# Output projection of a differential-attention layer as seven block products over token pairs, column halves and the two k-tiles of a head

## The reference

```python
mod = silu(c) @ ada_w + ada_b; shift, scale, gate = split(mod, 3)
h = rms_norm(x, norm_pre) * (1 + scale) + shift
q, k, v, z = h @ w_in                    # 8 heads, v 256 wide, q and k 2 x 128 wide
p = softmax(where(mask, q k^T / sqrt(128), -1e30))      # for each of two maps
o = (p[0] - lam * p[1]) @ v              # mask: key chunk <= query chunk (64)
o = rms_norm(o, subln) * 0.8 * silu(z)   # per head
y = o @ w_out                            # 1024 x 2048 times 2048 x 2048
out = x + gate * rms_norm(y, norm_post)
```

## Time and profile before

| | |
|---|---|
| three executions | 1976.6, 1975.08, 1976.04 us; median 1976.04 |
| the profiled execution, its own time | 1976.31 us |
| its span, first to last instruction | 1974.5 us |
| mean granted TensorE clock | 0.994 |
| TensorE busy | 98% of the span |
| HBM read / written | 295.75 / 128.98 MB |

### The profile page before, as it was taken

One profiled execution on the slowest core, in us unless ns is written; L12 is line 12 of the kernel. 1 busy time (PEld: TensorE's weight loads), 2 busy tenths in 40 slices (PEclk: granted clock), 3 DMA queues, 4 the chain that ended last, 5 costly groups with the idle time before them and its releaser, 6 DMA issues.

```text
span 1974.5 us, 26574 instructions
## 1 busy us (share of the span) xinstructions
PE 1927.3 (98%) x9222; PEld 1579.9 (80%) x9222; DVE 1294.4 (66%) x2118; ACT 787.2 (40%) x1567; POOL 567.1 (29%) x624
## 2 busy tenths in 40 slices
PE   4999999999999999999999999999999999999998
PEld 1378888888888888888888888888888878888886
DVE  2776766666556446788788888888788745434352
ACT  4533333333444333444444444444444434322240
POOL 2033333423456324232332434332332310000000
PEclk8999999999999999999999999999999999999999
DMA  9777666563556777776768687777768675377453
GB/s 327 249 242 238 211 195 214 189 215 103 183 177 216 273 275 257 234 251 208 242 195 261 203 241 229 233 238 217 238 200 257 234 256 171 112 256 210 153 154 85
DMA packets 398353, 426.51 MB, mean 216 GB/s; under 512 B 21158, under 2 KB 295692, under 8 KB 396044
## 3 DMA queue, kind: packets, MB, share of 16 engines
q1 hardware_dynamic: 397936, 424.77, 67.8%
q10 hardware_dynamic: 284, 0.05, 0.0%
HBM read 295.75 MB, written 128.98 MB: 215 GB/s over the span
## 4 chain that ended last, share of the span: by engine, by line
PE 89%; SPq 3%; DMA 2%; DVE 2%; POOL 2%; issue 1%; ACT 1%; DVEq 0%; POOLq 0%; ACTq 0%
PE ps L1620 28%; PE ps L1622 28%; PE ps L1621 28%; PE ps L1752 2%; PE ps L1603 1%; POOL stg L766 1%; PE ps L1726 1%; POOL sums L745 1%; SPq L507 1%; PE ps L1771 1%; DMA h_dr<-stg 1%; PE ps L1588 1%; SPq L393 1%; DMA q_sb<-q_dr 0%; DMA x2s<-in_x_dram 0%
## 5 line engine op out<-in xcount | busy, mean ns | idle before, releaser
L1620 PE MATMUL ps<-blk,ring 128*128 128x512 f32 x1524 | 602.8, 396 | 5.8 <-issue 2.3
L1622 PE MATMUL ps<-blk,ring 128*128 128x512 f32 x1524 | 594.1, 390 | 0.0
L1621 PE MATMUL ps<-blk,ring 128*128 128x512 f32 x1524 | 593.7, 390 | 0.0
L1620 PEld LDWEIGHTS ps<-blk,ring 128*128 128x128 f32 x1524 | 286.3, 188 | 64.6 <-issue 6.8
L1622 PEld LDWEIGHTS ps<-blk,ring 128*128 128x128 f32 x1524 | 286.0, 188 | 60.8
L1621 PEld LDWEIGHTS ps<-blk,ring 128*128 128x128 f32 x1524 | 286.5, 188 | 55.8
L1149 DVE TENSOR_TENSOR ring<-sums,ring 128x512 fp32r<-128x512 f32 x256 | 225.8, 882 | 127.7 <-ACT ring L849 125.4
L745 POOL TENSOR_TENSOR sums<-raw 128x512 f32<-128x512 f32 x128 | 192.8, 1506 | 346.7 <-DVE ring L1149 262.8
L849 ACT ACTIVATE ring<-sums 128x512 fp32r<-128x512 f32 x256 | 160.0, 626 | 173.5 <-PE ps L1622 171.3
L1149 DVE TENSOR_TENSOR ring<-raw,ring 128x512 fp32r<-128x512 f32 x192 | 163.6, 853 | 80.9 <-ACT ring L849 79.8
L745 POOL TENSOR_TENSOR sums<-sums,raw 128x512 f32<-128x512 f32 x128 | 190.5, 1488 | 24.8 <-DVE ring L1149 17.7
(11 more groups left out here) (161 smaller groups left out, 3039.4 us busy)
## 6 DMA issues: line engine op xcount, KB each, us to landing
raw<-in_diff_w_in_dram SPq DMA_DIRECT2D x64, 1024.0 KB, 7.2
w_raw<-in_diff_w_out_dram SPq DMA_DIRECT2D x128, 256.0 KB, 3.9
d_dr<-cc SPq DMA_DIRECT2D x124, 256.0 KB, 2.7
cc<-d_dr SPq DMA_DIRECT2D x124, 256.0 KB, 3.9
ada<-in_ada_w_dram SPq DMA_DIRECT2D x92, 256.0 KB, 7.1
ada<-in_ada_w_dram SPq DMA_DIRECT2D x32, 512.0 KB
q_sb<-q_dr SPq DMA_DIRECT2D x64, 256.0 KB, 3.2
k_sb<-k_dr SPq DMA_DIRECT2D x64, 256.0 KB, 3.9
```

Of the source, the lines that this page charges most:

```text
L1620: MM(dst, a_hi, b_hi, start=start, stop=False, skip_group_check=True)
L1621: MM(dst, a_hi, b_lo, start=False, stop=False, skip_group_check=True)
L1622: return MM(dst, a_lo, b_hi, start=False, stop=stop, skip_group_check=True)
```

## The change

The output projection is written as block products over pairs of token tiles (2p and 2p+1), halves of 512 columns inside each column half c of 1024, and the two k-tiles of a head. With A the gated output of a head in blocks (token tile, k-tile) and B a head's rows of `w_out` in blocks (k-tile, 512 columns), each head needs seven products:

- P1 = A11 B11, P2 = A12 B21, P3 = (A12 - S2) B22, P4 = A22 T4, P5 = S1 T1, P6 = S2 T2, P7 = S3 T3
- S1 = A21 + A22, S2 = S1 - A11, S3 = A11 - A21
- T1 = B12 - B11, T3 = B22 - B12, T2 = B22 - T1, T4 = B21 - T2
- Y11 = P1 + P2, Y12 = P1 + P6 + P5 + P3, Y22 = P1 + P6 + P7 + P5, Y21 = P1 + P6 + P7 + P4

A unit is one product of one head for all four token pairs, again 12 matmuls of 128x512. The table `OUT` gives the order: per column half P1, P6, P7, P4, P5, P3, P2, each over the heads. P6, P7, P4 and P3 go on in the bank of the product before (`GOES_ON`); after P1, P6, P7 and P4 the bank is copied to `y` by ScalarE (p even) and VectorE (p odd), after the others VectorE adds the bank to `y`. In the first column half the last head is left out of the seven and done as eight plain products (K11, K12, K21, K22, two units each). So there are 7 x 7 + 8 + 7 x 8 = 113 units.

The sums S are made by POOL (`o_sums`, four 128x128 operations per pair, in all heads) and stored unsplit with A in `s_dr` (`store_pair`); the splits and stores of `oz` are gone. The sums T are made by POOL in place (`t_sum`, four 128x512 operations per head and column half) and stored in `t_dr`: for c = 0 in the first half of the input products, one head per 14 products, for c = 1 in the last head's attention (`T_AT`) and after it. The load of x's second half comes after the first of these passes, from product 116 on. A unit's two operands, weights and A, 128x512 each, are loaded together into one of `UR` = 10 buffers and split together, 128x1024 (`unit_high`, L1114; `unit_low`, L1526), `made_by(u) - u` units ahead: 2 until unit 38, rising to 8 from unit 59 on. The squares are taken from `y`, and POOL multiplies `y` by `gpb` (`L927`). In the last product (P2 of c = 1) TensorE goes pair by pair, 24 matmuls each.

```diff
-    OUTS = 2 * GROUPS * KT
...
+    PAIRS = TT // 2
+    K12, K11, K21, K22 = range(NP, NP + 4)
+    OUT = [(0, (P1,), 0), (0, (P6,), 0), (0, (P7,), 0), (0, (P4,), 0), (0, (P5,), 0), (0, (P3, K12), 0),
+           (0, (P2, K11), 1), (0, (K21,), 0), (0, (K22,), 1),
+           (1, (P1,), 0), (1, (P6,), 0), (1, (P7,), 0), (1, (P4,), 0), (1, (P5,), 1), (1, (P3,), 1), (1, (P2,), 0)]
+    GOES_ON = (P6, P7, P4, P3)
+    COPIED = (P1, P6, P7, P4)
+    TO = {P1: (0, 0), P2: (0, 0), P6: (0, 1), P3: (0, 1), P7: (1, 1), P5: (1, 1), P4: (1, 0), K21: (1, 0), K22: (1, 1)}
+    UNIT = [(q, c, op, u) for q, (c, ops, _) in enumerate(OUT) for op in ops
+            for u in range(2 if op >= NP else HEADS - (c == 0))]
+    OUTS = len(UNIT)
+    BEGIN = [min(n for n in range(OUTS) if UNIT[n][0] == q) for q in range(len(OUT))]
+    END = [max(n for n in range(OUTS) if UNIT[n][0] == q) for q in range(len(OUT))]
+    LAST = len(OUT) - 1
...
+    UR = 10
+    LEAD = 2
...
+    T_AT = {0: 0, 2: 1, 3: 2, 4: 3, 5: 4, 6: 5, 7: 6}
...
+        def made_by(n):
+            return min(OUTS - 1, n + LEAD + min(6, max(0, (n - BEGIN[5]) // 4))) if n >= 0 else n + LEAD
...
+            def store_pair(h, p):
+                sp.wait_ge(ozf_ok, h * NB + 2 * p + 2)
+                sp.dma_start(s_dr[0:4, h, :, p].rearrange("o p n -> p o n"),
+                             ozf.rearrange("p i m n -> p (i m) n")).then_inc(s_st, 16)
+                sp.wait_ge(osum_ok, 4 * (h * PAIRS + p + 1))
+                sp.dma_start(s_dr[4:8, h, :, p].rearrange("o p n -> p o n"), osum[:, :, :]).then_inc(s_st, 16)
...
+            def load_unit(n):
...
+                    sp.wait_ge(unit_used, n - UR + 1)
+                if op in (P5, P7, P4, P6):
+                    t = (P5, P7, P4, P6).index(op)
+                    sp.wait_ge(t_st[u % 2], 32 * ((c * HEADS + u) // 2 + 1))
+                    src = t_dr[c, u, t]
...
+                sp.dma_start(ubf[k][:, 1, 0], src).then_inc(unit_in[k], 16)
+                if op >= NP:
+                    s, h = 2 * (op in (K21, K22)) + u, LH
+                else:
+                    s, h = {P1: 0, P2: 1, P4: 3, P5: 4, P6: 5, P7: 6, P3: 7}[op], u
+                sp.wait_ge(s_st, 32 * PAIRS * (h + 1))
+                sp.dma_start(ubf[k][:, 1, 1], s_dr[s, h].rearrange("p t n -> p (t n)")).then_inc(unit_in[k], 16)
...
+            while n < BEGIN[5] + HEADS - 1:
+                load_unit(n)
+                n += 1
+            store_t(1, HEADS - 2)
+            load_t(1, HEADS - 1)
+            store_pair(LH, PAIRS - 1)
+            while n < OUTS:
+                load_unit(n)
+                n += 1
+                if n == BEGIN[6]:
+                    store_t(1, HEADS - 1)
+                t, r = divmod(n - BEGIN[9] - UR, 4)
+                if r == 0 and 0 <= t < TT:
+                    if t == 0:
+                        for e in range(2):
+                            sp.wait_ge(t_st[e], 32 * HEADS)
+                    load_x(XT[t])
...
+            def o_sums(a):
+                n = 4 * (a // 2)
+                a11, a12, a21, a22 = ozf[:, 0, 0], ozf[:, 0, 1], ozf[:, 1, 0], ozf[:, 1, 1]
+                pool.wait_ge(ozf_ok, a + 1)
+                TTP(osum[:, 0], a21, a22, ALU.add).then_inc(osum_ok, 1)
+                TTP(osum[:, 2], a11, a21, ALU.subtract).then_inc(osum_ok, 1)
+                pool.wait_ge(osum_ok, n + 1)
+                TTP(osum[:, 1], osum[:, 0], a11, ALU.subtract).then_inc(osum_ok, 1)
+                pool.wait_ge(osum_ok, n + 3)
+                TTP(osum[:, 3], a12, osum[:, 1], ALU.subtract).then_inc(osum_ok, 1)
...
+                if qb == NB - 1:
+                    o_sums(HEADS * NB - 1)
+                if qb in T_AT:
+                    for step in range(4):
+                        t_sum(1, T_AT[qb], step)
...
+            def unit_high(n):
+                act.wait_ge(unit_in[n % UR], 32 * (n // UR + 1))
+                A(ub[n % UR][:, 0], ubf[n % UR][:, 1], ACT.Copy).then_inc(unit_hi, 1)
+            def make(u):
+                for n in range(made_by(u - 1) + 1, made_by(u) + 1):
+                    unit_high(n)
...
+            def read_out(q, p):
+                to, bank = y_block(q, p), ps[:, out_bank(q, p)]
+                dve.wait_ge(*made(q, p))
+                if OUT[q][1][0] in COPIED:
+                    i = V.tensor_copy(to, bank)
...
-            def tiles_done(u):
+                    c, ops, _ = OUT[q]
+                    old = max(r for r in range(q) if OUT[r][0] == c and TO[OUT[r][1][0]] == TO[ops[0]])
+                    dve.wait_ge(*read[old, p])
+                    i = TTV(to, bank, to, ALU.add)
+                i.then_inc(y_d, 1)
...
+            def unit(n, p):
+                q, c, op, u = UNIT[n]
+                new = n == BEGIN[q] and OUT[q][1][0] not in GOES_ON
+                s = slice(p * P, (p + 1) * P)
+                return three(ps[:, out_bank(q, p)], ub[n % UR][:, 0, 1, s], ub[n % UR][:, 1, 1, s],
+                             ub[n % UR][:, 0, 0], ub[n % UR][:, 1, 0], new, n == END[q])
+            def bank_waits(q, p):
+                if on_bank[q] is not None:
+                    pe.wait_ge(*read[on_bank[q], p])
+                elif p == 0 and q:
+                    pe.wait_ge(ozf_ok, HEADS * NB)
+                elif p == 0:
+                    pe.wait_ge(ev_d, 3 * GP + NP * GP)
...
+            def tick(n):
+                q = UNIT[n][0]
+                pe.wait_ge(unit_ok, n + 1)
+                for p in range(PAIRS):
+                    if n == BEGIN[q]:
+                        bank_waits(q, p)
+                    last = unit(n, p)
+                    if n == END[q] and p < PAIRS - 1:
+                        last.then_inc(op_done, 1)
+                last.then_inc(unit_used, 1)
...
+            for p in range(PAIRS):
+                read_out(LAST, p)
+                col = (2 + TO[P2][1]) * HALF
+                dve.wait_ge(*read[LAST, p])
+                TTV(y_end[:, p], y_block(LAST, p), gpb[:, col:col + HALF], ALU.mult).then_inc(y_end_ok, 1)
+                if p == 0:
+                    finish(1, PAIRS - 1)
+                y_sum(0, slice(p, p + 1), SQ[LAST, p] + 1)
+                finish(0, p)
```

More of the change, by code:

```diff
@@ L86, in build @@
     ADA_BUF = list(range(14)) + [0, 1, 2, 3, 4, 5, 6, 7, 8, 9, 0, 1, 2, 3, 4, 5, 0, 1]
-    assert GC == UK * P
-    assert END[EARLY] >= sum(map(sum, SLOTS)) > END[EARLY - 1]
+    T_PASS = 14
+    assert BEGIN[6] > sum(map(sum, SLOTS)) + 8 and OUT[6][2] == 1
     ctx = ExitStack()
@@ L220, in build @@
+        y_end = at("y_end", [P, PAIRS, HALF], F32, [e_at + BLK // 2 * 3])
+        assert (OUTS - HEADS - 1) % UR == 4 and max(x_places) + BLK // 2 <= nc.sbuf_usable_end
+        for used in (base, a_at, b_at, z_at):
             assert used[0] <= nc.sbuf_usable_end, (used[0], nc.sbuf_usable_end)
@@ new lines, in _ @@
+            while n < OUTS:
[4 more added lines that the diff above has]
+                t, r = divmod(n - BEGIN[9] - UR, 4)
+                if r == 0 and 0 <= t < TT:
+                    if t == 0:
+                        for e in range(2):
+                            sp.wait_ge(t_st[e], 32 * HEADS)
+                    load_x(XT[t])
+            for p in range(PAIRS):
+                t = 2 * p + 1
+                sp.wait_ge(fin, 2 * p + 2 if p < PAIRS - 1 else 2 * PAIRS)
+                sp.dma_start(out[0, t * P:(t + 1) * P, :], xt[t][:, :]).then_inc(out_st, 16)
@@ L719, in _ @@
+            for p in range(PAIRS):
+                t = 2 * p
+                for k, (b, e) in enumerate(((0, 1024), (1536, 2048), (1024, 1536))):
+                    sp.wait_ge(fin, 2 * PAIRS + 3 * p + k + 1)
+                    sp.dma_start(out[0, t * P:(t + 1) * P, b:e], xt[t][:, b:e]).then_inc(out_st, 16)
+            sp.wait_ge(out_st, 4 * PAIRS * 16)
         @block.gpsimd
@@ new lines, in tick, with y_sum, finish @@
+            def tick(u):
+                if u in END:
+                    q = END.index(u)
+                    for p in range(PAIRS):
+                        if read[q, p][0] is y_d:
+                            read_out(q, p)
+            def y_sum(i, pairs, done):
+                dve.wait_ge(yss_ok, done)
+                V.tensor_reduce(out=yms[:, i, pairs], in_=yss[:, i, pairs], axis=AX.X, op=ALU.add).then_inc(yms_ok, 1)
+            def finish(i, p):
+                t = 2 * p + i
+                if i == 1 and p == 0:
+                    dve.wait_ge(xh_in, 16 * TT)
+                dve.wait_ge(yrs_ok, 1 if i else p + 2)
+                dve.wait_ge(yg_ok, SQ[LAST - 2 if i else LAST - 1, p] + 1)
+                r = yrs[:, i, p:p + 1]
+                if not i:
+                    dve.wait_ge(y_end_ok, p + 1)
+                for k, src in enumerate((y[0][:, t], y[1][:, t]) if i else
+                                        (y[0][:, t], y[1][:, t, HALF:2 * HALF], y_end[:, p])):
+                    col = slice(k * 2 * HALF, (k + 1) * 2 * HALF) if i else (
```

(9 more changed lines are left out.)

557 lines of the change are left out of this document (224 added, 333 removed).

## The result

The changed kernel takes **1998.1 us** (median of 4 runs, 1994.8 to 2007.6) against 1975.6 us beside it (4 runs, 1974.0 to 1976.6): a ratio of 1.0122, 95% interval 1.0103 to 1.0142. It is slower by 1.2%. Forecast were 1961.0 us and a range up to 1972; slower had a chance of 0.04. The prediction was wrong. The profiled execution took 1999.6 us, its span is 1997.8.

A forecast was written before the change was run, and what follows sets the result against it. The prediction took the kernel to be a TensorE matmul stream, thin only in the last head's first attention rounds and the tail: 1976.3 - 40.8 + 9 + 6.5 + 5 + 5 = 1961.0 us, range 1945 to 1972.

The forecast's parts named there:

- Matmuls removed: Output projection: 113 units instead of 128, 15 units at 2.72 us saved on TensorE, -40.8 us.
- Ahead of the output stage: Input products: added POOL sums, loads and stores make TensorE wait for nothing, 0 us (-1 to +4).
- Attention rounds: Last head's attention: 1024-wide splits delay the links TensorE waits for, +9 us (+2 to +16).
- its 1.5 for POOL: Last head's attention: POOL's second-half sums in rounds 1, 3 and 4 can hold a VectorE operation, 1.5 us.
- The queue at unit 42: Plain products needing the last token pair: its store waits behind second-half traffic, TensorE stands 5.6 us; +6.5 us (+3 to +11).
- Changes of block: Units 64, 72, 80 and 96: a split made ahead delays the bank's read-out, +5 us (0 to +9).
- L - 3: Block changes: TensorE's wait given a unit load of L us; L about 4.2, so 1.2 us.
- The tail: After the last matmul: VectorE arrives at the last pair 2 to 6 us late, +5 us (+0.5 to +8).
- POOL and VectorE lock at every meeting: Rival for rounds and tail: each meeting costs a full sum, 8 + 4 us more, 1973 us; chance 0.10.
- Slower, by DMA: Rival: the queue gives under 210 GB/s and paces the unit stream, +22, about 1983 us; chance 0.05.
- The clock falls again and again: Rival: five more half-speed dips at TensorE's waits cost 9 us, about 1970 us; chance 0.13.
- my high bounds: Whole kernel: all terms at their upper limits, with +4 for the early part, give 1983 us.

The follow-up runs named there:

- early_lead6: Changed kernel with second-half sums made in the first half of the input products and splits at most 6 units ahead: 1957.2 us, 0.9909 of the kernel before.
- run 4: Changed kernel with splits at most 6 units ahead of TensorE instead of 8 (8 again from unit 98): 1986.3 us, 1.0045 of the kernel before.
- run 6: Changed kernel with all POOL second-half sums, but only two blocks loaded and none stored: 1978.4 us, 1.0011 of the kernel before.

## Why the prediction was wrong, by its own steps

**Matmuls removed, -40.8: right.** With nothing in its way the rest takes 216.7 us (early_lead6): 79 units at 2.72 are 214.9, and one wait of 0.8 and a turn lie in it.

**Ahead of the output stage, 0: right,** +0.5 us.

**Attention rounds, +9: they cost 24.3.** The links that I costed are there. Without the second half's sums the rounds take 9.0 us more than before, where my sum without its 1.5 for POOL was 7.5. What failed is the sentence that gives POOL's sums 1.5 us, and that the same sums' loads and stores have no term at all. That these sums and their traffic are the cause is not in doubt: five traces of the rounds without them lie at 141 to 143 us, and the three with all of them and the loads at their old places at 159 to 165. How the 15 us divide is less sure: in one profiled execution each, sums alone cost 7.5 and traffic alone 11.7. I counted the sums in rounds 1, 3 and 4; they run in rounds 5, 6 and 7 as well, and these three, which I had called hidden, lost 7.4 us of the 24.3 (1.2 without the sums and their traffic). I had followed the queue at unit 42 and not in the rounds, where the next unit's load stands behind 1 MB of stores and 1 MB of loads and its split is made only two units ahead of its use. I also counted the old split outputs' loads as a gain of 1 and left out what comes instead.

**The queue at unit 42, +6.5: 16.0** (10 units and a turn, 27.4 us, took 43.4). The chain was right in its order, and most of its links too short. Counted from the last weighted sum's end, forecast and measured: gate done +6.5 and +8.0, since two splits and four read-outs (L1526, L1543) stand ahead of the scaled output; the four sums of 128x128 2.0 and 5.7 us, at 1.4 each beside VectorE's splits and 0.45 alone; issued at +16 and +22.7; landed in 5.5 and 6.7 us. The four 128x512 sums (5.4) and the splits at the end (2.4) were right, and the last load took 2.6 us where I had 3.7. TensorE was there at +23.7, so it waited 10.6 us and 1.0 more before unit 44, instead of 5.6; the slow clock took 2.4 where I had put 0.9, and 0.8 is a wait for the read-out of a bank behind unit 34.

**Changes of block, +5: 15.2** by run 4 (15.9 counted unit by unit in the change's own trace). The formula, L - 3, holds to 0.1 us at three changes: L was 4.2, 6.0 and 6.0 us and the waits 1.2, 3.0 and 3.0. I took L as 4.2 everywhere from a quiet stretch and gave it 5.3 at most. And I put no price on the clock: 6 us of the 15.2 are no waits. At the fourth change the wait was 2.1 us, forecast 1.8.

**The tail, +5: 8.4.** VectorE is late from the first pair on, not only at the last. Its first additions took 8.2 us instead of 5.1, which is the 3 us missing.

**The rivals.** "POOL and VectorE lock at every meeting", chance 0.10, describes what happened in the rounds (7.5 us), at unit 42 (3.7) and in the tail (3.1): about 14 us against the 12 that I worked out, and more if the medians of run 6 are right for the rounds. The tail's part is read from durations alone: no run takes POOL's products away. The case against it, that most of VectorE's lines read SBUF once, counted lines and not time: the splits are half of VectorE's work there and read it twice. It is the rule of the Trainium skill ("SBUF — State Buffer", Who interferes with whom), and run 6 agrees with it: the splits' mean rises from 1259 to 1419 ns when POOL's sums come back without their traffic. "Slower, by DMA" looked for the queue's limit in the pure stage, where it is not (216.7 us with all of x's traffic), and not in the rounds. "The clock falls again and again", 9 us by my count, came true as well: some 2.4 behind unit 42 and 6 behind the block changes. I had treated as alternatives four mishaps that add up, with one cause behind most of them, operands that arrive just in time. That made the range too narrow, but it is not all: my high bounds together give only 1983, and the rounds, unit 42, the changes of block and the tail all passed their own (16, 11, 9 and 8 us).
